# Differential attention's first two output pairs and its last residual quarter transposed by trips instead of TensorE; linear attention's gates moved in the order tables

## The reference

```python
def gla_mixer(h, w_in, w_gate_f, b_gate_f, w_gate_b, b_gate_b, g_out, w_out):
    q, k, v, r, zf, zb = split_cols(h @ w_in, [...])
    la_f = heads(jax.nn.log_sigmoid((zf @ w_gate_f + b_gate_f).astype(F32)) / GLA_TAU, GLA_HK)
    la_b = heads(jax.nn.log_sigmoid((zb @ w_gate_b + b_gate_b).astype(F32)) / GLA_TAU, GLA_HK)
    ...

def diff_attn_mixer(h, pos, w_in, g_q, g_k, ..., g_sub, w_out, lambda_init):
    q, k, v = split_cols(h @ w_in, [D_MODEL, D_MODEL, D_MODEL])
    ...
        s = jnp.einsum('bhtqd,bhtkd->bhtqk', q_blk, kt).astype(F32) * scale
        pr = jax.nn.softmax(s, axis=-1)
        a = pr[:, :, 0] - lam * pr[:, :, 1]
        return jnp.einsum('bhqk,bhkd->bhqd', a.astype(vt.dtype), vt)
    ...
    o = rms_norm(o, g_sub) * (1.0 - lambda_init)
    return o.reshape(bsz, seq, D_MODEL) @ w_out
```

## Time and profile before

| | us |
|---|---|
| median of three runs | 898.39 (897.45 to 898.75) |
| profiled execution | 898.01 |
| its span in the trace | 896.2 |
| PE busy in the span | 890.2 (99%) |
| DVE busy | 659.3 (74%) |
| ACT busy | 503.0 (56%) |
| GpSimd (POOL) busy | 71.2 (8%) |
| `wlo` on DVE, 295 of them | 346.9 |
| `whi` on ACT, 295 of them | 302.5 |

### The profile page before, as it was taken

One profiled execution on the slowest core, in us unless ns is written; L12 is line 12 of the kernel. 1 busy time (PEld: TensorE's weight loads), 2 busy tenths in 40 slices (PEclk: granted clock), 3 DMA queues, 4 the chain that ended last, 5 costly groups with the idle time before them and its releaser, 6 DMA issues.

```text
span 896.2 us, 12091 instructions
## 1 busy us (share of the span) xinstructions
PE 890.2 (99%) x4344; PEld 735.3 (82%) x4344; DVE 659.3 (74%) x1009; ACT 503.0 (56%) x822; POOL 71.2 (8%) x88
## 2 busy tenths in 40 slices
PE   9999999999999999999999999999999999999998
PEld 8978888888888888778888888888888888887777
DVE  6885478776746588997787777655779987779764
ACT  6656555444445476878564444434765445577581
POOL 0000110000000113211010000000010000115200
PEclk9999999999999999999999999999999999999999
DMA  7953448766677665433377676775678775757501
GB/s 259 339 171 129 151 164 310 268 244 240 244 255 239 209 235 196 157 118 100 117 269 270 240 249 243 269 234 182 211 267 285 238 245 175 281 174 246 185 31 48
DMA packets 80356, 190.20 MB, mean 212 GB/s; under 512 B 7012, under 2 KB 34532, under 8 KB 80296
## 3 DMA queue, kind: packets, MB, share of 16 engines
q1 hardware_dynamic: 78840, 185.61, 60.1%
q0 software_dynamic: 1024, 3.15, 1.0%
q10 hardware_dynamic: 432, 0.66, 0.2%
HBM read 173.14 MB, written 16.25 MB: 211 GB/s over the span
## 4 chain that ended last, share of the span: by engine, by line
PE 96%; DVE 2%; ACT 1%; DMA 1%; issue 0%
PE bank L1826 86%; PE bank L1864 2%; PE bank L1879 1%; PE bank L2134 1%; PE bank L2160 1%; PE bank L2239 1%; PE bank L2269 1%; DVE wlo L1099 1%; DMA h<-x_dram 1%; PE bank L2145 0%; PE bank L2225 0%; PE bank L2037 0%; PE bank L2041 0%; PE bank L2249 0%; PE bank L2120 0%; PE bank L1845 0%
## 5 line engine op out<-in xcount | busy, mean ns | idle before, releaser
L1099 DVE TENSOR_TENSOR wlo<-raw,whi 128x1024 fp32r<-128x1024 f32 x295 | 346.9, 1214 | 43.3 <-ACT whi L694 42.6
L694 ACT ACTIVATE whi<-raw 128x1024 fp32r<-128x1024 f32 x295 | 302.5, 1060 | 128.0 <-PE bank L1826 108.1
L1826 PE MATMUL bank<-whi,x_hi 128*128 128x512 f32 x560 | 152.5, 394 | 0.0
L1826 PE MATMUL bank<-wlo,x_hi 128*128 128x512 f32 x560 | 149.8, 389 | 0.0
L1826 PE MATMUL bank<-whi,x_lo 128*128 128x512 f32 x560 | 149.8, 389 | 0.0
L1826 PEld LDWEIGHTS bank<-wlo,x_hi 128*128 128x128 f32 x560 | 105.1, 188 | 22.2
L1826 PEld LDWEIGHTS bank<-whi,x_lo 128*128 128x128 f32 x560 | 105.1, 188 | 22.0
L1826 PEld LDWEIGHTS bank<-whi,x_hi 128*128 128x128 f32 x560 | 103.5, 188 | 22.6 <-issue 1.8
L1826 PE MATMUL bank<-whi,y_hi 128*128 128x512 f32 x396 | 107.6, 393 | 0.1
L1826 PE MATMUL bank<-wlo,y_hi 128*128 128x512 f32 x396 | 106.0, 389 | 0.0
L1826 PE MATMUL bank<-whi,y_lo 128*128 128x512 f32 x396 | 106.0, 389 | 0.0
(11 more groups left out here) (254 smaller groups left out, 906.6 us busy)
## 6 DMA issues: line engine op xcount, KB each, us to landing
raw<-stream_dram SPq DMA_DIRECT2D x295, 512.0 KB, 4.5
ffn_blocks<-ffn_blk SPq DMA_DIRECT2D x22, 256.0 KB, 2.2
ffn_land<-ffn_blocks SPq DMA_DIRECT2D x22, 256.0 KB, 4.5
residual_blocks<-h_blk SPq DMA_DIRECT2D x17, 256.0 KB, 2.0
h_land<-residual_blocks SPq DMA_DIRECT2D x17, 256.0 KB, 2.9
cv_blocks<-cv_blk SPq DMA_DIRECT2D x7, 256.0 KB, 4.5
cv_land<-cv_blocks SPq DMA_DIRECT2D x7, 256.0 KB, 3.4
h_blocks<-h_blk SPq DMA_DIRECT2D x3, 512.0 KB, 3.0
```

Source lines behind the costliest of these rows:

```text
L694: A(whi[:, u % RING, :], raw[:, u % SLOTS, :], ACT.Copy).then_inc(sem("w_hi"), 1)
L1099: V.tensor_tensor(wlo[:, u % SLOTS, :], raw[:, u % SLOTS, :], whi[:, u % RING, :].bitcast(F32), ALU.subtract).then_inc(sem("w_lo"), 1)
L1826: last = T.matmul(bank[pair + t][:, :], lhs[a][:, kt, t * P:(t + 1) * P], w[:, place(w, u), kk * NW:(kk + 1) * NW], start=part != 1 and k ...
```

## The change

Four things are changed, and nothing of what is computed.

1. **The gates.** In `GLA_ORDER`, ACT's steps "expabs" and "ln" go from unit 5 to 6 and from 5 to 7, DVE's "gates" and "ln" from 4 to 5 and from 5 to 7. PE's table for this stage is the same.
2. **Input of differential attention, kt 6 and 7.** They come by a trip, "df q1". DVE transposes blocks right behind the residual addition, SP has the trip ahead of unit 10 of the stage, ACT and DVE split the landed tile behind the weights up to some unit 8. PE issues four transposes there instead of eight. The first two tiles are interleaved (`ORDERS[DF_IN]`): units 0 to 2 are the first tile's, unit 3 the second's, unit 4 reads kt 6, 7 for the first tile, and units 5 to 7 end the second.
3. **The first two output pairs.** They come by trips "dfo q0" and "dfo q1". PE's steps "pair" 0 and 1 go, DVE gets "turn" (the block transpose of `df_o`, for pair 0 behind softmax step 5 and for pair 1 behind the pair's normalising) and "ylo", ACT "yhi". SP has the trips ahead of units 33 and 35 of the stage. Blocks and landed tiles (`blocks`, `landed`; branches of theirs for names that no trip has are left out below) use the four quarters of the buffer `df_tok` (`dtok`), which the queries and keys had before.
4. `pair_hi` and `pair_lo` are handed the gain as a function, since the output pairs have another gain than the norms.

```diff
-PIECES = (... "gate0 t0", "gate0 t1", "mix1 h1", ...
+PIECES = (... "gate0 t0", "gate0 t1", "df q1", "dfo q0", "dfo q1", "mix1 h1", ...
...
+ORDERS[DF_IN] = ((0, 0), (0, 1), (0, 2), (1, 0), (0, 3), (1, 1), (1, 2), (1, 3))
...
 def done_at(tile):
-    return END[tile + 1] + (2 if tile in PAIRED else 0)
+    return END[tile + 1] + (2 if tile in PAIRED else 1 if tile == DF_IN else 0)
...
-        (5, "expabs", 0), (5, "ln", 0), ...
+        (6, "expabs", 0), (7, "ln", 0), ...
...
+        oblk = dtok[:, :, :, :].rearrange("p a t n -> p (a t n)").rearrange("p (s n) -> p s n", s=4)
+        oland = dtok[:, :, :, :].rearrange("p a t n -> p (a t n)").rearrange("p (s i n) -> p s i n", s=4, i=P // B)[:, 2:4]
+
+        def blocks(name):
...
+            return (oblk if name[:3] == "dfo" else sblk)[:, slot(name), :]
+
+        def landed(name):
...
+            return (oland if name[:3] == "dfo" else sland)[:, slot(name), :, :]
...
@@ trips
-                    sp.dma_start(s_dram[n], sblk[:, q, :]).then_inc(sem(f"g_out{q}"), 16)
+                    sp.dma_start(s_dram[n], blocks(name)).then_inc(sem(f"g_out{q}"), 16)
...
-                    sp.dma_start(sland[:, q, :, :], s_dram[n].rearrange("q n -> (q n)")
+                    sp.dma_start(landed(name), s_dram[n].rearrange("q n -> (q n)")
...
                 fetch(done, END[out_tile])
                 done = END[out_tile]
+                if n == 1:
+                    done = trips(END[DF_OUT] + 9, "dfo q0")
+                    done = trips(END[DF_OUT] + 11, "dfo q1")
...
+                if n == 0:
+                    done = trips(END[DF_IN] + 10, "df q1")
...
@@ ACT: ple
                 if n == 0:
-                    lhs_hi(Y, norm_gain(j + 1), (6, 7))
+                    lhs_hi(Y, norm_gain(j + 1), (6,))
                 squares(j + 1, 1)
+                if n == 0:
+                    split_to(END[DF_IN] + 2 + AHEAD)
+                    pair_hi(norm_gain(j + 1), Y, "df q1", 6)
...
@@ ACT: differential attention
+                elif step == "yhi":
+                    pair_hi(lambda kt: cols[:, C_DF:C_DF + 1], X, f"dfo q{arg}", 2 * arg)
...
@@ DVE: ple
                     elif n == 0:
-                        split_to(END[DF_IN] + 1 + AHEAD)
-                        lhs_lo(dst, norm_gain(j + 1), (6, 7))
+                        pair_blk("df q1", 12 * n + 10, 6, True)
+                        split_to(END[DF_IN] + AHEAD)
+                        lhs_lo(dst, norm_gain(j + 1), (6,))
+                        split_to(END[DF_IN] + 2 + AHEAD)
+                        pair_lo(norm_gain(j + 1), dst, "df q1", 6)
...
@@ DVE: differential attention
+                elif step == "turn":
+                    dve.wait_ge(sem("df_y"), arg + 1)
+                    pair_blk(f"dfo q{arg}", 0, 2 * arg, False, src=do)
+                elif step == "ylo":
+                    pair_lo(lambda kt: cols[:, C_DF:C_DF + 1], X, f"dfo q{arg}", 2 * arg)
...
@@ PE: differential attention
-            df_half0, df_pairs = list(half) + [None, None], [None] * 4
+            df_half0, df_pairs = list(half) + [None, piece_need("df q1")], [piece_need("dfo q0"), piece_need("dfo q1"), None, None]
...
                     if step == "second":
-                        df_half0[2:4] = h_T(1, 3)
+                        pe.wait_ge(sem("h_new"), 12)
+                        df_half0[2:3] = lhs_T(h, (6,))
...
-            product(DF_IN, Y, "df_in", need=df_half0, beside=df_beside)
-            for t in range(1, 6):
+            first_tiles(DF_IN, Y, "df_in", df_half0, df_beside)
+            for t in range(2, 6):
                 product(DF_IN + t, Y, "df_in", beside=df_beside)
```

More of the change, by code:

```diff
@@ L135 @@
     "dve": (
-        (4, "zT", 0), (4, "tile", 1), (5, "z4", 0), (4, "gates", 0), (5, "ln", 0), (9, "tile", 2),
+        (4, "zT", 0), (4, "tile", 1), (5, "z4", 0), (5, "gates", 0), (7, "ln", 0), (9, "tile", 2),
         (10, "cumulate", 0), (11, "cumulate", 1), (13, "far", 0), (15, "scores", 0), (16, "far", 1),
@@ L157 @@
         (20, "tile", 4), (20, "scores", 4), (20, "aT", 2), (20, "scores", 5), (20, "aT", 3), (21, "av", 1),
-        (21, "scores", 6), (21, "aT", 4), (24, "scores", 7), (24, "pair", 0), (24, "tile", 5), (24, "av", 3),
-        (24, "aT", 5), (25, "aT", 6), (26, "av", 5), (26, "aT", 7), (26, "pair", 1), (27, "av", 7), (28, "pair", 2),
+        (21, "scores", 6), (21, "aT", 4), (24, "scores", 7), (24, "tile", 5), (24, "av", 3),
+        (24, "yhi", 0), (24, "aT", 5), (25, "aT", 6), (26, "av", 5), (26, "aT", 7), (27, "av", 7), (27, "yhi", 1), (28, "pair", 2),
         (28, "pair", 3),),
@@ L439, in _ @@
                 SOURCE[n + 1], SOURCE[n + 2] = n + 2, n + 1
-            for tile in PAIRED:
+            for tile in PAIRED + (DF_IN,):
                 for n, (t, k) in enumerate(order_of(tile)):
@@ L709, in norm_gain, with pair_hi @@
                 return lambda kt: cols[:, C_NORM + j * KT + kt:C_NORM + j * KT + kt + 1]
-            def pair_hi(j, dst, name, kt0):
+            def pair_hi(gain, dst, name, kt0):
                 q = slot(name)
@@ L716, in pair_hi @@
                     A(dst[0][:, kt0 + k, :].rearrange("p (t i b) -> p t i b", t=TT, b=B),
-                      sland[:, q, :, :].rearrange("p i (k t b) -> p k t i b", k=2, t=TT)[:, k], ACT.Copy,
-                      scale=norm_gain(j)(kt0 + k)).then_inc(sem("g_hi"), 1)
+                      landed(name).rearrange("p i (k t b) -> p k t i b", k=2, t=TT)[:, k], ACT.Copy,
+                      scale=gain(kt0 + k)).then_inc(sem("g_hi"), 1)
             def mixer_lhs(j, dst, out):
@@ L1130, in residual, with pair_blk @@
                                     bank[2 * (tile % 2) + t][:, :], ALU.add).then_inc(sem("h_new"), 1)
-            def pair_blk(name, news, kt0, first):
+            def pair_blk(name, news, kt0, first, src=h):
                 if turn(name) > 1:
@@ L1139, in pair_blk, with pair_lo @@
                     at = slice(kt0 * P, (kt0 + 2) * P)
[L1140 to L1141 removed]
+                    last = V.transpose(blocks(name).rearrange("p (f k t b) -> p t f k b", f=P // B, k=2, t=TT)[:, t],
+                                       src[:, t, at].rearrange("p (k b f) -> p f k b", b=B, f=P // B))
                 last.then_inc(sem("g_blk"), 1)
[L1144 removed]
+            def pair_lo(gain, dst, name, kt0):
                 n = piece(name)
```

39 lines of the change are left out of this document (21 added, 18 removed), and 4 rows, old and new, of the table DF_ORDER.

## The result

The changed kernel takes 905.68 us, the median of five runs (903.05 to 905.99); the kernel before takes 898.75 us (897.45 to 900.09). The ratio is 1.007 (95% interval 1.0054 to 1.0085): slower by 0.7%. I had forecast 902.1 us with a range of 899.6 to 904.9. The direction was right and the time was missed, by 0.8 us over the range and 3.6 us over the forecast. The profiled execution is the quickest of the five, 903.05 us with a span of 901.2; its mean granted clock of TensorE is 0.998. One of the others has 0.996 and 904.65 us, three have 0.994 and 905.7 to 906.0 us. The execution profiled of before has 1.000. So the trace alone would have hidden more than half of the miss.

A forecast was written before the change was run, and what follows sets the result against it. TensorE's own program was taken to bound the kernel, busy 890.2 of 896.2 us. 898.01 - 1.23 - 0.29 - 0.87 + 3.8 + 2.3 = 901.7, plus 0.38 to the median: 902.1 us, range 899.6 to 904.9.

The forecast's parts named there:

- gates: Linear-attention gates: reordering ACT and DVE steps removes PE's waits of 1.03 and 0.2 us, -1.23 us.
- input product: Differential attention's first input product: four transposes fewer, -0.49, and a new wait, +0.20; together -0.29 us.
- two output pairs: Output pairs 0 and 1 of differential attention: PE loses two times four transposes, -0.87 us.
- first pause: Before unit 24, PE waits for pair 0's trip and ACT's copies: +3.8 us (3.6 to 4.8).
- second pause: Before unit 26, PE waits for ACT's copies of pair 1, behind the last heads' evacuation: +2.3 us (2.1 to 2.5).
- clock behind them: Rival: TensorE's clock drops to 1.2 GHz behind the 3.8 us pause, up to 904.9 us; chance 0.15.
- the logarithm's price of one `whi`: Gates: one extra ACT `whi` delays the logarithm 1.06 us, leaving 0.17 us of slack at PE's cumulation; taken at nothing.
- late `y_lo`: Input product, ninth matmul of unit 2: PE waits 0.20 us for `y_lo`, with unknown ends of 0 and 0.49.
- the gates did bring their gain: Rival denied here: the gates bring nothing because slack is missing or a weight lands late, 903.3 us; chance 0.10.
- the second pause was there: Rival denied here: ACT reaches pair 1's copies in time, so no pause before unit 26, 899.8 us; chance 0.07.
- the trips were not hidden: Rival denied here: the trips are hidden behind PE's work, the change gains 2.4 us, 896.0 us; chance 0.08.

The follow-up runs named there:

- e10_again: The changed kernel run again with no edit, on another chip, for one more trace; 906.36 us in its single execution.
- e6_gates: The kernel before with only the gates' steps moved to the changed kernel's places; median 896.99 us, ratio 0.9985 to the kernel before.
- e3_yhi: The changed kernel with ACT's copies of output pair 1 ahead of the evacuation of heads 6 and 7; median 902.77 us, ratio 1.0041 to the kernel before.
- e1_same: The changed kernel run again with no edit, four executions; median 906.05 us, ratio 1.0082 to the kernel before.
- e9_twice: The kernel before with six PE pauses added in the second SwiGLU and no trip; median 920.68 us, ratio 1.0258 to the kernel before.
- e2_fill: The changed kernel with 14 unused matmuls in PE's first pause and 6 in its second; median 903.19 us, ratio 1.0056 to the kernel before.

## Why the prediction was right and wrong

The terms of the sum, in the changed kernel's trace (a shift is the start of an instruction in it less that in before's):

| step | forecast | measured | from |
|---|---|---|---|
| gates | -1.23 | -1.36 | shift from -0.21 ahead of them to -1.57 behind |
| input product | -0.29 | -0.07 | -1.62 (331.26 to 329.64) to -1.69 (412.85 to 411.16, where the pair's transposes stood) |
| two output pairs | -0.87 | -0.87 | four transposes each, as the earlier trace rows |
| first pause | +3.8 | +3.97 | `av` to unit 24: 5.68 (411.16 to 416.84), not 1.71 |
| second pause | +2.3 | +2.30 | `av` to unit 26: 4.00 (427.29 to 431.29), not 1.70 |
| clock behind them | 0 | +1.6 (+4.2 in e10_again) | 4.42 for unit 24, not 2.83 |

The prediction's pauses are shifts of a unit's start, so they are measured in the same way here. The brackets of PE's waits, 3.74 and 2.06, are smaller by 0.23, since the rows of the `av` products (1.95 us) reach beyond the 1.70 us at which the next matmul could have started. With the shift of -0.21 at the start the terms add up to +5.4; the spans differ by 5.0, and the other 0.3 goes between 634.21 us, where the shift is +5.34, and 748.94, where it is +5.04; nothing was changed there, and I can't place it.

**The gates** went as worked out: the logarithm's price of one `whi`, a slack of 0.28 us at the cumulation (0.17 forecast), and both pauses gone. e6_gates shows it alone. The 0.21 us of shift ahead of them were there before any changed step, and no term stands for them.

**The input product** was right in direction and too large. Four transposes fewer gave 0.43, not 0.49. The late `y_lo` took 0.23 before the ninth matmul of unit 2 (0.20 forecast), and the group behind that wait took 0.11 more than before (334.92 to 335.96 is 1.04, not 0.93), for which the sum had no term. So -0.13 is left at 335.96, and -0.07 at the output pairs; where the rest went I can't place.

**The pauses** were right in place, releaser and size: the second to 0.01 us and step by step (ACT's evacuation 1.98 us behind the start of `av`, its copies 1.07 behind that, PE 0.95 behind them), the first to 0.2 us. There PE started 0.25 us behind the end of ACT's copies (416.59 to 416.84), where 0.05 was taken. The first chain is that of the prediction: transposes, DMA out, DMA back, ACT. The second was a wait in ACT's order and nothing else, which e3_yhi took away by one exchange of steps.

**The clock is the step that failed.** The prediction had it at nothing in the sum, and as a rival, "no row shows such a fall", with a chance of 0.15 and a price of at most 2.8 us, for one pause. The clock fell behind the first pause in all three traces of the changed kernel (this one, e1_same, e10_again) and cost 1.5 to 2.6 us there, so the price of one fall was bounded rightly. But in two of the three it fell again behind the second pause, for another 1.6 us, and that fall no term, rival or bound had. So the chance was too low, and the upper end of 904.9 too. That the trace of before shows no fall was evidence for nothing: it has no pause over 1.03 us behind the start. The right reading would have been that a pause of 3.8 us lies outside all that before's rows cover, so that both levels were open, and a rule from elsewhere was the only guide. The Trainium skill, "TensorE: Matmul & The Clock Gate", section "Why this matters for your kernels", warns of such gaps; the traces agree for the first pause (granted clock 0.50 behind 3.74 us), and so the rival deserved a far higher chance than 0.15. They don't agree throughout: the clock stayed up behind 3.52 us in e9_twice, and fell behind 2.06 us in two traces, which is shorter than the gaps of that warning. With 4.2 us for the clock in place of 0, as the one trace with a mean clock of 0.994 has it, the sum is 902.1 + 4.2 = 906.3, and most executions lie at 905.5 to 906.7; without it e2_fill's three undisturbed executions lie at 901.9 to 902.3.

The other rivals: the gates did bring their gain, the second pause was there, and the trips were not hidden. The late landing of a trip, which no rival had, appears in one trace, and in none of the changed kernel.

## What to carry to other kernels

Price a pause of the bounding engine as the pause plus what its clock may lose behind it, once for every pause, and where the trace of before has no pause of that length, take its silence as no evidence. A transpose by a trip is free only if block and reader lie more than the trip's whole length (here 6 us from the start of the block transposes to ACT's copy) of the bounding engine's work apart; four transposes taken from that engine just before the reader gave 0.43 us, and the pause in their place cost 2.3 and 4.0. In an in-order engine, look for what stands ahead of the copy as well as for the data: one exchange of two steps was worth 3.3 us.
